# Gate and up projections of feed-forward tiles 3 to 20 as seven block products instead of eight

## The chip, the cores and the metric

The kernel runs on one core of one Trainium2 chip. The metric is the device time of one execution in microseconds (us).

## The reference, cut to what matters

Two encoder layers are computed for 576 tokens (512 of a prompt and 64 of a sample) of width 1024. Each layer has two feed-forward networks (FFNs), with a mixer and a cross attention between them. Only the FFNs are touched:

```
def swiglu(x, w_gate, w_up, w_down):
    return (jax.nn.silu(x @ w_gate) * (x @ w_up)) @ w_down

x = layer_norm(ALPHA * x + 0.5 * swiglu(x, ffn1_gate, ffn1_up, ffn1_down), g[0], b[0])
...
x = layer_norm(ALPHA * x + 0.5 * swiglu(x, ffn2_gate, ffn2_up, ffn2_down), g[3], b[3])
```

D_MODEL is 1024 and D_FF 2816, all in fp32.

## The kernel before, in words

Activations lie transposed, features on the partitions and the 576 tokens on the free axis, in halves of 288 (HT). Every fp32 operand is split into a rounded part hi and a rest lo, and a product is three matmuls: hi by hi, hi weights by lo tokens, lo weights by hi tokens (`passes`, L394, and `passes_half`, L406, for one half). Weights come as units of 128x1024, in one stream by SP into the ring `w_raw` of three buffers (L2226). SP loads a buffer again once its unit is split. Pool splits every unit (`unit`, L2124): one TENSOR_SCALAR writes the hi part (L2135), four TENSOR_TENSORs the lo part (L2142), into one of 12 slots. `unit_done` tells Pool that a slot is free, `unit_split` tells PE that a unit is there.

An FFN has 22 tiles of 128 hidden features and 66 units: a gate and a up unit for each tile, and two down units for two tiles. There are three stages:

- **Head** (`head`, L457): tiles 0 to 2, first for token half 0, then for half 1, while VectorE (DVE) and ScalarE (ACT) still normalise half 1. Its banks are those of `pairD` and one each of `pairA` and `pairB`.
- **Bodies** (`ffn`, L562): a tile is a `proj` of gate into pairA (48 matmuls of 288 columns) and one of up into pairB (48). ACT takes the silu of the gate, DVE multiplies it with up (L1591), ACT rounds the hidden tile to hi (L1103), and DVE makes its lo (L1595). Between two tiles stands a `down` of 96 matmuls over the two tiles before, in eight groups of 12 that alternate between pairD0 and pairD1. DVE adds each group to `y` (L1609).
- **Tail** (`tail`, L472): tile 21 and the last two down products by token half. Then `norm_of_ffn` runs: ACT squares `y`, Pool sums the squares (`squares_sum`, L2157), and `stats` (L586) on PE averages the sums over the partitions, between the gate and the up product of half 1.

What sets the order is the order of the program on each engine, with semaphores between them. Pool's is:

```
                ffn_units(0)
                units(mix, mix + HEAD)
                squares_sum(0, 0)
                squares_sum(0, 1)
```

so that before the squares of an FFN come the last units of its tail and the first six of the stage behind it. Only after the last FFN do none follow.

## Time and profile before

| | |
|---|---|
| median of three runs | 2674.93 us (2664.05 to 2677.69) |
| span of the profiled execution | 2675.5 us (no other time of that execution is given) |
| PE busy | 2556.2 us (96%), 18450 matmuls |
| DVE busy | 1056.0 us (39%) |
| ACT busy | 583.9 us (22%) |
| Pool busy | 1542.6 us (58%) |
| granted TensorE clock, mean | 0.972 of full speed |

The span runs from the first instruction to the last. Busy time is the union of an engine's instructions, and matmuls overlap: one lasts about 299 ns in the record, while they start closer together than that. The last section of rows gives what the argument needs, in groups with numbers.

### The profile page before, as it was taken

The page shows a single profiled execution, that of the slowest core. Times are in us where ns is not written, and L with a number is a line of the kernel's source. Part 1 is how long each engine was busy: PE and PEld are TensorE (multiplying, and loading weights), DVE is VectorE, ACT ScalarE, POOL GpSimd, SP SyncE. Part 2 cuts the span into 40 slices and gives each one's busy share as a digit, 9 for nine tenths or more (in the row PEclk, how much of TensorE's full clock was granted, in tenths as well). Part 3 has the DMA queues.
Part 4 walks back from the last instruction along what each step waited for, and adds up shares of the span by engine and source line. Part 5 has one row for each costly group of instructions (what it writes and reads, how often), then busy time and mean ns, then how long its engine had stood idle before and what let it go on. Part 6 is the DMA issues. An engine that isn't in the chain of part 4 may idle for free.

```text
span 2675.5 us, 47942 instructions
## 1 busy us (share of the span) xinstructions
PE 2556.2 (96%) x18450; PEld 2444.5 (91%) x18450; DVE 1056.0 (39%) x1601; ACT 583.9 (22%) x1096; POOL 1542.6 (58%) x1877
## 2 busy tenths in 40 slices
PE   8999999999988899999999999999999879999997
PEld 7999999978767799999999999999787768999997
DVE  3222225654647622222422222256445575222224
ACT  2000004422315500000320000044223254000004
POOL 8866662733239686666486666626332588766641
PEclk9999999989979999999999999999889999999999
DMA  6322220212113132222132222202121121322201
GB/s 229 118 79 86 79 86 9 80 48 71 52 48 95 57 113 81 85 80 84 40 114 87 83 82 80 83 2 87 40 89 35 64 97 64 103 87 78 85 33 36
DMA packets 61099, 203.99 MB, mean 76 GB/s; under 512 B 6808, under 2 KB 13976, under 8 KB 60312
## 3 DMA queue, kind: packets, MB, share of 16 engines
q1 hardware_dynamic: 52288, 184.83, 21.3%
q10 hardware_dynamic: 8664, 17.17, 1.8%
q8 instruction: 96, 1.57, 0.2%
q14 instruction: 51, 0.42, 0.1%
HBM read 195.66 MB, written 7.88 MB: 76 GB/s over the span
## 4 chain that ended last, share of the span: by engine, by line
PE 84%; DVE 9%; POOL 3%; issue 3%; ACT 1%; DMA 0%; DVEq 0%; POOLq 0%; ACTq 0%
PE pairA L401 22%; PE pairD L401 20%; PE pairB L401 19%; PE pairD L410 8%; PE pairA L410 2%; PE pairB L410 2%; POOL scratch L2175 1%; PE pairD L671 1%; PE pairD L673 1%; POOL w L2142 1%; DVE prx L2098 1%; DVE scratch L1816 1%; DVE y L1634 1%; PE pairD L793 0%; PE pairB L828 0%
## 5 line engine op out<-in xcount | busy, mean ns | idle before, releaser
L2142 POOL TENSOR_TENSOR w<-w_raw,w 128x256 fp32r<-128x256 f32 x1372 | 1044.2, 792 | 28.6
L2135 POOL TENSOR_SCALAR w<-w_raw 128x1024 fp32r<-128x1024 f32 x343 | 365.3, 1065 | 808.3 <-issue 450.0
L401 PE MATMUL pairA<-x_hi,w 128*128 128x288 f32 x3136 | 570.3, 299 | 3.6 <-DVE scratch L1564 2.7
L401 PE MATMUL pairB<-x_hi,w 128*128 128x288 f32 x2752 | 497.1, 298 | 0.0
L401 PE MATMUL pairD<-h_hi,w 128*128 128x288 f32 x2688 | 481.0, 298 | 16.0 <-DVE kw L1906 6.3
L401 PEld LDWEIGHTS pairA<-x_hi,w 128*128 128x128 f32 x3136 | 473.9, 191 | 7.0 <-issue 6.1
L401 PEld LDWEIGHTS pairD<-h_hi,w 128*128 128x128 f32 x2688 | 403.8, 191 | 18.9 <-issue 8.4
L401 PEld LDWEIGHTS pairB<-x_hi,w 128*128 128x128 f32 x2752 | 413.9, 191 | 1.1 <-issue 0.2
L1609 DVE TENSOR_TENSOR y<-y,pairD 128x576 f32<-128x576 f32 x256 | 193.1, 754 | 561.6 <-PE pairD L401 561.6
L401 PE MATMUL pairA<-x_lo,w 128*128 128x288 f32 x1568 | 339.1, 298 | 0.0
L401 PE MATMUL pairB<-x_lo,w 128*128 128x288 f32 x1376 | 297.2, 298 | 0.0
L401 PE MATMUL pairD<-h_lo,w 128*128 128x288 f32 x1344 | 290.6, 298 | 0.0
L1103 ACT ACTIVATE h_hi<-scratch 128x576 fp32r<-128x576 f32 x72 | 49.4, 686 | 956.5 <-DVE scratch L1591 956.5
L401 PEld LDWEIGHTS pairA<-x_lo,w 128*128 128x128 f32 x1568 | 256.2, 191 | 0.0
L401 PEld LDWEIGHTS pairB<-x_lo,w 128*128 128x128 f32 x1376 | 223.7, 191 | 0.0
L401 PEld LDWEIGHTS pairD<-h_lo,w 128*128 128x128 f32 x1344 | 218.3, 190 | 0.0
L2175 POOL TENSOR_TENSOR scratch<-scratch 128x288 f32<-128x288 f32 x112 | 98.6, 880 | 192.9 <-ACT scratch L1120 188.9
L410 PE MATMUL pairD<-x_hi,w 128*128 128x288 f32 x832 | 175.7, 303 | 22.0 <-DVE w L1520 12.4
L1591 DVE SCALAR_TENSOR_TENSOR scratch<-scratch,pairB 128x576 f32<-128x576 f32 x72 | 54.0, 751 | 339.8 <-PE pairB L401 339.8
L410 PEld LDWEIGHTS pairD<-x_hi,w 128*128 128x128 f32 x832 | 138.0, 192 | 24.9 <-issue 19.6
L410 PE MATMUL pairD<-h_hi,w 128*128 128x288 f32 x768 | 158.4, 298 | 2.3 <-DVE h_lo L1770 2.3
L410 PEld LDWEIGHTS pairD<-h_hi,w 128*128 128x128 f32 x768 | 124.6, 188 | 4.7 <-DVE h_lo L1770 3.2
(340 smaller groups left out, 2925.0 us busy)
## 6 DMA issues: line engine op xcount, KB each, us to landing
w_raw<-in_stream SPq DMA_DIRECT2D x348, 512.0 KB, 3.4
out_ak<-pa ACTq DMA_DIRECT2D x2, 1152.0 KB, 4.7
out_y<-y SPq DMA_DIRECT2D x8, 288.0 KB, 2.2
mem_raw<-in_mem ACTq DMA_DIRECT2D x2, 1024.0 KB, 4.7
cst<-in_consts ACTq DMA_DIRECT2D x1, 1740.0 KB, 8.2
tb_dram<-in_rel ACTq DMA_DIRECT2D x2, 768.0 KB
y<-in_x ACTq DMA_DIRECT2D x2, 576.0 KB, 7.0
y<-in_x ACTq DMA_DIRECT2D x1, 1152.0 KB, 11.2
```

The costliest lines, as they stand in the source:

```text
L401: ins.append(mm(out[0:m, half, 0:n], wt, mv_[:, c:c + n], start=(start and i == 0), stop=(stop and i == 2)))
L410: return [mm(out[:, 0:HT], wt, mv_[:, c], start=(start and i == 0), stop=(stop and i == 2)) for i, (wt, mv_) in enumerate(((wh, hi), (wh, ...
L671: i = mm(o[m, cols], lhs, dT[:, h, tok], start=True, stop=(t == 0))
L673: i = mm(o[m, cols], cs[r, p, st, 0:w], qw[r, p, tok], start=False, stop=True)
L1103: f(hs[t % 4][0], hf[:, 0:TOK], ACT.Copy).then_inc(h_hi_done.sem, 1)
L1591: v.scalar_tensor_tensor(out=both(hf[:, 0:TOK]), in0=both(sil[t % 2][:, 0:TOK]), scalar=0.5, in1=B.halves(), op0=ALU.mult, op1=ALU.mult).t ...
L1609: v.tensor_tensor(both(y[:, n]), both(y[:, n]), pair.halves(), ALU.add)\
L1634: v.scalar_tensor_tensor(out=y[:, n, half(h)], in0=y[:, n, half(h)], scalar=scalar, in1=t[:, 0:HT], op0=ALU.mult, op1=ALU.add).then_inc(us ...
L1816: step(v.reciprocal(r_, r_))
L2135: pool.tensor_scalar(hi, w_raw[:, j], 1.0, 0.0, ALU.mult, ALU.add).then_inc(unit_hi, 1)
L2142: i_ = pool.tensor_tensor(lo[:, b], w_raw[:, j, b], hi[:, b].bitcast(F32), ALU.subtract)
L2175: pool.tensor_tensor(s2[:, c], a[:, c], sil[n % 2][:, c], ALU.add)\
```

## The change

For tiles 3 to 20 of each FFN the gate and up products become one two-by-two block product. The weights have the blocks A11 and A12 (rows 0 to 511 and 512 to 1023 of gate) and two of up, the tokens are cut by rows and by token halves, and seven products of 12 matmuls on 288 columns take the place of eight. Four of the weight blocks are sums (S1 to S4), four of the token blocks too (T1 to T4, made once for an FFN). One call of `tile_pair` issues the seven products P1 to P7 of one tile, in the order of its `part` calls; P5, P6 and P7 add to the banks of P1, P3 and P4.

- **DVE** makes the weight sums of each tile (4 operations of 128x512), the lo parts of all seven blocks (7 of 128x512), five combinations of the products (128x288, one operand in PSUM), the hidden tile and its lo. It still adds the down groups. Its order is that of `half_body(k)`, which covers tiles t = 2k+3 and r = 2k+4. The sums and lo parts of tile t+2 stand within tile r, those of tile r within tile t and the down.
- **ACT** rounds the seven blocks to hi (7 of 128x512), copies P1 out of its bank (`keep_m1`), and takes silu by halves.
- **Pool** splits only the down units of the bodies, head and tail units as before. `pair_split` waits for DVE's three lo parts of the raw blocks, then releases both raw buffers.
- The homes of split weights change: two sets of seven blocks for alternating tiles, two slots for down units. Four of the six tail units lie over T1 to T4 and wait for the last products of tile 20.
- The loads of `gw_raw` and `lru_w` move from the first FFN to its norm, since they share memory with the blocks.

```diff
--- before.py
+++ after.py
-SLOTS = 12
-HEAD, TAIL, BODY = 6, 6, 12
-BODIES = (FFN_UNITS - HEAD - TAIL - 6) // BODY
...
+A11, S2, S1, S3, A12, S4, A22 = range(7)
+SUMS = (S1, S3, S2, S4)
+T2, T1, T3, T4 = range(4)
+SETS = (("e0", "e1", "e2", "sc", "b0", "b1", "b2"), ("b3", "b4", "b5", "b6", "b7", "b8", "b9"))
+D_SLOTS, TAIL_SLOTS = (5, 8), (9, 8, 10, 11, 12, 13)
+TAIL_OVER = {62: 2, 63: 3, 64: 4, 65: 7}
...
+    ffn = list(range(HEAD)) + HALVES * ["x", "x", *D_SLOTS, "y", "y"] + list(TAIL_SLOTS)
+    mixer = [i if i < HEAD else (i - HEAD) % 5 for i in range(MIX_UNITS + X_UNITS - 3)] + [HEAD - 1, 6, 7]
...
+                def tile_pair(u, t, fi, off=0):
+
+
+                    q = fi * PAIRS + t - 3
+                    at = pair_counts(l, q, off)
+                    first = t == 3
+                    blocks = sets[(t - 3) % 2]
+                    x_ = [[(x_hi[:, 4 * k:4 * k + 4, h * HT:h * HT + HT], x_lo[:, 4 * k:4 * k + 4, h * HT:h * HT + HT])
+                           for h in range(2)] for k in range(2)]
+
+                    def part(bank, b, src, start):
+                        (wh, wl), (hi, lo) = blocks[b], src
+                        ins = []
+                        for k in range(4):
+                            for i_, (wt, mv_) in enumerate(((wh, hi), (wh, lo), (wl, hi))):
+                                ins.append(mm(bank.t[:, 0:HT], wt[:, k], mv_[:, k], start=(start and k == i_ == 0),
+                                              stop=(k == 3 and i_ == 2), skip_group_check=not start))
+                        ins[-1].then_inc(product.sem, 1)
+                        return ins[0]
+
+                    unit_there(u + 1, BODY * off)
+                    if not first:
+                        pe.wait_ge(gate_on.sem, at(gate_on, 2, -1))
+                    tell_over(part(A.bank[0], A11, x_[0][0], True))
+                    if first:
+                        pe.wait_ge(tx_ready.sem, tx_ready.value(l, 4 * fi + 4))
+                    else:
+                        pe.wait_ge(combined.sem, at(combined, 5, -4))
+                    pe.wait_ge(sum_lo.sem, at(sum_lo, 4, 3))
+                    part(A.bank[1], S2, tx[T2], True)
+                    if not first:
+                        pe.wait_ge(combined.sem, at(combined, 5, -1))
+                    part(B.bank[0], S1, tx[T1], True)
+                    if not first:
+                        pe.wait_ge(combined.sem, at(combined, 5, 0))
+                    part(B.bank[1], S3, tx[T3], True)
+                    pe.wait_ge(m1_kept.sem, at(m1_kept, 1, 1))
+                    part(A.bank[0], A12, x_[1][0], False)
+                    pe.wait_ge(sum_lo.sem, at(sum_lo, 4, 4))
+                    pe.wait_ge(combined.sem, at(combined, 5, 2))
+                    part(B.bank[0], S4, x_[1][1], False)
+                    pe.wait_ge(combined.sem, at(combined, 5, 3))
+                    part(B.bank[1], A22, tx[T4], False)
+                    units_over(2)
...
                     with pe.Fori(0, BODIES) as i:
                         for m in range(2):
                             u = u0 + 12 + 6 * m
-                            proj(u, A, None, 12 * i, 4 * i, a0 + 2 * m)
-                            proj(u + 1, B, None, 12 * i, 4 * i, b0 + 2 * m)
+                            tile_pair(u, 5 + 2 * m, fi, i)
                             down(u + 2, h0 + 7 + 2 * m, None, 4 * i, 8 * i, (d0 + 4 * m, d1 + 4 * m), slot=2 - 2 * m)
-                            proj(u + 4, A, None, 12 * i, 4 * i, a0 + 2 * m + 1)
-                            proj(u + 5, B, None, 12 * i, 4 * i, b0 + 2 * m + 1)
...
                     hi_half(fi, FT - 1, 1)
+                    if fi == 0:
+                        load_mixer()
...
+                    y_ = [[y[:, 4 * k:4 * k + 4, half(h)] for h in range(2)] for k in range(2)]
+                    raw = tx_f
+                    inc(v.tensor_tensor(raw[T1], y_[0][0], y_[0][1], ALU.subtract), tx_made)
+                    inc(v.tensor_tensor(raw[T3], y_[0][1], y_[1][1], ALU.subtract), tx_made)
+                    dve.wait_ge(tx_made.sem, tx_made.value(l, 4 * fi + 1))
+                    inc(v.tensor_tensor(raw[T2], y_[1][1], raw[T1], ALU.add), tx_made)
+                    dve.wait_ge(tx_made.sem, tx_made.value(l, 4 * fi + 3))
+                    inc(v.tensor_tensor(raw[T4], y_[1][0], raw[T2], ALU.subtract), tx_made)
...
+                def sums(fi, t, first, off=0):
+
+                    u = fi * FFN2_AT + 2 * t + 2 * ((t - 3 + 1) // 2)
+                    at = pair_counts(l, fi * PAIRS + t - 3, off)
+                    g, up = raw_pair(u)
+                    raw = sums_f[(t - 3) % 2]
+                    if first == 0:
+                        raw_there(dve, l, u, off)
+                        raw_there(dve, l, u + 1, off)
+                        room(dve, l, u, off)
+                        v.tensor_tensor(raw[S1], up[:, 0:4], up[:, 4:8], ALU.add).then_inc(sum_made.sem, 1)
+                        v.tensor_tensor(raw[S3], g[:, 0:4], up[:, 0:4], ALU.add).then_inc(sum_made.sem, 1)
+                    else:
+                        dve.wait_ge(sum_made.sem, at(sum_made, 4, 1))
+                        v.tensor_tensor(raw[S2], raw[S1], g[:, 0:4], ALU.add).then_inc(sum_made.sem, 1)
+                        dve.wait_ge(sum_made.sem, at(sum_made, 4, 3))
+                        v.tensor_tensor(raw[S4], raw[S2], g[:, 4:8], ALU.add).then_inc(sum_made.sem, 1)
...
+                    m6, m5, m7 = (b.t[:, 0:HT] for b in (A.bank[1], B.bank[0], B.bank[1]))
+                    if n == 0:
+                        dve.wait_ge(m1_kept.sem, at(m1_kept, 1, 1))
+                    dve.wait_ge(product.sem, at(product, 7, (2, 3, 4, 6, 7)[n]))
+                    if n in (1, 2):
+                        dve.wait_ge(combined.sem, at(combined, 5, n))
...
+                    out, a, b, op = ((v_, m6, kept, ALU.subtract), (up1, v_, m5, ALU.subtract), (up1, up1, m7, ALU.add),
+                                     (g1, m5, v_, ALU.subtract), (up0, v_, m7, ALU.add))[n]
+                    v.tensor_tensor(out, a, b, op).then_inc(combined.sem, 1)
...
                 def ffn(fi, h0):
                     for h in range(2):
                         for t in range(3):
+                            if (h, t) == (0, 2):
+                                tokens_made(fi)
                             hidden_half(fi, t, h)
-                    a0, b0 = uses[("ffn", fi, "A")], uses[("ffn", fi, "B")]
+                            if (h, t) == (0, 2):
+                                tokens_lo(fi)
+                            if (h, t) == (1, 0):
+                                sums(fi, 3, 0)
+                                sums(fi, 3, 2)
+                            if (h, t) == (1, 1):
+                                raws_lo(fi, 3, (0, 1, 2))
+                                for n in range(4):
+                                    sums_lo(fi, 3, n)
...
+                    def half_body(k, off=0):
+                        t, r = 2 * k + 3, 2 * k + 4
+                        more = k + 1 < HALVES
+                        combine(fi, t, h0, 0, off)
+                        combine(fi, t, h0, 1, off)
+                        combine(fi, t, h0, 2, off)
+                        if k:
+                            sums(fi, r, 0, off)
+                            raws_lo(fi, r, (0, 1), off)
+                        combine(fi, t, h0, 3, off)
+                        if k:
+                            sums(fi, r, 2, off)
+                        combine(fi, t, h0, 4, off)
+                        hidden(fi, t, off)
+                        if k == 0:
+                            hidden_lo(fi, t, h0, off)
+                            sums(fi, r, 0)
+                            raws_lo(fi, r, (0, 1))
+                            sums(fi, r, 2)
+                        for n in range(KT):
+                            down_add(k, n, off)
+                            if n == 1:
+                                if k:
+                                    hidden_lo(fi, t, h0, off)
+                                raws_lo(fi, r, (2,), off)
+                            if 2 <= n < 6:
+                                sums_lo(fi, r, n - 2, off)
+                        if more:
+                            sums(fi, t + 2, 0, off)
+                        combine(fi, r, h0, 0, off)
+                        if more:
+                            sums(fi, t + 2, 2, off)
+                        combine(fi, r, h0, 1, off)
+                        combine(fi, r, h0, 2, off)
+                        if more:
+                            raws_lo(fi, t + 2, (0, 1, 2), off)
+                        combine(fi, r, h0, 3, off)
+                        if more:
+                            sums_lo(fi, t + 2, 0, off)
+                        combine(fi, r, h0, 4, off)
+                        if more:
+                            sums_lo(fi, t + 2, 1, off)
+                        hidden(fi, r, off)
+                        if more:
+                            sums_lo(fi, t + 2, 2, off)
+                        hidden_lo(fi, r, h0, off)
+                        if more:
+                            sums_lo(fi, t + 2, 3, off)
...
+                    if SLOT[w] in TAIL_SLOTS[2:]:
+                        pool.wait_ge(product.sem, product.value(l, 7 * ((w // FFN2_AT + 1) * PAIRS - 1)
+                                                                + TAIL_OVER[w - w // FFN2_AT * FFN2_AT]))
...
+                def pair_split(u, fi, t, off=0):
+
+                    at = pair_counts(l, fi * PAIRS + t - 3, off)
+                    pool.wait_ge(raw_lo.sem, at(raw_lo, 3, 3))
+                    pool.wait_ge(unit_split, l * UNITS + u + BODY * off)
+                    pool.sem_inc(unit_split, 2)
...
+                    def half_body(k, off=0):
+                        u = at + HEAD + HALF * k
+                        pair_split(u, fi, 2 * k + 3, off)
+                        unit(u + 2, off)
+                        unit(u + 3, off)
+                        pair_split(u + 4, fi, 2 * k + 4, off)
```

Three places in the order of the instructions follow. First VectorE inside the loop, in the second tile of a half body, behind its last raw lo part. `e` and `w` are homes of blocks, `sc_lo` too, `e_0f` and `w_0f` the unrounded sums, and `scratch` holds the combinations and the hidden tile (L1853). Now:

```order
L1846 TENSOR_TENSOR scratch<-pairB,scratch 128x288 [waits product]
L1815 ISA
L1817 TENSOR_TENSOR e<-e_0f,e 128x512 [waits block_hi]
L1846 TENSOR_TENSOR scratch<-scratch,pairB 128x288 [waits product]
L1815 ISA
L1817 TENSOR_TENSOR sc_lo<-scratch,sc_hi 128x512 [waits block_hi]
L1851 ISA
L1852 ISA [waits gate_on]
L1853 SCALAR_TENSOR_TENSOR scratch<-scratch 128x576 [waits combined]
L1815 ISA
L1817 TENSOR_TENSOR e<-e_0f,e 128x512 [waits block_hi]
L1858 ISA
```

The second L1846 waits for P7, and the third L1817 makes the lo part of S2 for the next tile. Before, DVE had here only L1591 and L1595.

Second PE, at the start of the next tile, the products P1 and P2 (`tq` are the token sums). Now:

```order
L674 ISA [waits unit_split]
L667 MATMUL pairA<-x_hi,e 128x288 [waits gate_on]
...
L679 ISA
L680 ISA [waits combined]
L667 MATMUL pairA<-tq,e 128x288 [waits sum_lo]
L667 MATMUL pairA<-tq,e 128x288 x11
L683 ISA
```

P2 begins when the lo part of S2 is there. Before, the gate product of a tile stood here, with one wait at its start.

Third Pool, from the end of its loop to the squares of the first norm. Now:

```order
L2470 TENSOR_SCALAR e<-w_raw 128x1024
L2477 TENSOR_TENSOR e<-w_raw,e 128x256 x4
L2470 TENSOR_SCALAR d<-w_raw 128x1024
L2477 TENSOR_TENSOR d<-w_raw,d 128x256 x4
L2470 TENSOR_SCALAR t<-w_raw 128x1024
L2477 TENSOR_TENSOR t<-w_raw,t 128x256 x4
...
L2470 TENSOR_SCALAR w<-w_raw 128x1024
L2477 TENSOR_TENSOR w<-w_raw,w 128x256 x4
...
L2527 TENSOR_TENSOR scratch<-scratch 128x288 x14
```

The t units are four and the w units six. Before, all twelve were w units in the same order; what moved is when their homes come free. The d unit (61) goes where the last down unit (57) was, which is free from P1 of tile 20 on, and behind it stand ten more units.

## Rows read from the trace of the kernel before

**Rows 1.** The page, part 1: busy time of the engines.
```profile
PE 2556.2 (96%) x18450; PEld 2444.5 (91%) x18450; DVE 1056.0 (39%) x1601; ACT 583.9 (22%) x1096; POOL 1542.6 (58%) x1877
```

**Rows 2.** Chain that ended last: start us, us, what. The downs of one FFN.
```profile
66.83 12.80 PE pairD L401 x96
105.17 12.80 PE pairD L401 x96
```

**Rows 3.** Stretch of a head: us, busy by PE, PEld, DVE, ACT, POOL, PEclk, DMA, GB/s.
```profile
1364.27:1377.07 12.80, 12.80 (x98) 12.80 (x97) 1.90 (x4) 1.72 (x4) 5.97 (x9) 1.00 0.18 53
```

**Rows 4.** Durations: by lines (mean ns after busy) or by source (ns min/median/max).
```profile
L1634 DVE SCALAR_TENSOR_TENSOR y<-y,pairD 128x288 f32<-128x288 f32 x128 | 54.3, 445 | 29.0 <-PE pairD L410 29.0
L1609 DVE TENSOR_TENSOR y<-y,pairD 128x576 f32<-128x576 f32 x256 | 193.1, 754 | 561.6 <-PE pairD L401 561.6
L1968 DVE TENSOR_TENSOR pc<-pc,scratch x8: 757/759/1186, 645.3 to 2132.0; 128x576 f32<-128x576 f32 x8
L1831 DVE TENSOR_TENSOR yd<-yd,scratch x4: 1109/1146/1186, 503.9 to 1858.5; 128x512 f32<-128x512 f32 x4
L2142 POOL TENSOR_TENSOR w<-w_raw,w x1372: 716/737/1720, 6.0 to 2583.5; 128x256 fp32r<-128x256 f32 x196
L1103 ACT ACTIVATE h_hi<-scratch 128x576 fp32r<-128x576 f32 x72 | 49.4, 686 | 956.5 <-DVE scratch L1591 956.5
```

**Rows 5.** Timeline of DVE at a tile's end: start us, us, what, [idle before].
```profile
309.81 0.76 DVE L1609 TENSOR_TENSOR y<-y,pairD 128x576 f32<-128x576 f32 x1 [0.84 <-PE pairD L401]
310.48 0.75 DVE L1591 SCALAR_TENSOR_TENSOR scratch<-scratch,pairB 128x576 f32<-128x576 f32 x1
311.98 1.30 DVE L1595 TENSOR_TENSOR h_lo<-scratch,h_hi 128x576 fp32r<-128x576 f32 x1 [0.75 <-ACT h_hi L1103]
```

**Rows 6.** Timeline of DVE, three heads, and of PE: tile 3.
```profile
35.37 0.60 DVE L1572 TENSOR_TENSOR h_lo<-scratch,h_hi 128x288 fp32r<-128x288 f32 x1 [0.51 <-ACT h_hi L1079]
...
927.68 0.60 DVE L1572 TENSOR_TENSOR h_lo<-scratch,h_hi 128x288 fp32r<-128x288 f32 x1 [0.51 <-ACT h_hi L1079]
...
948.27 0.50 PE L401 MATMUL pairA<-x_hi,w 128*128 128x288 f32 x2 [0.89 <-DVE scratch L1564]
...
1359.17 0.81 DVE L1572 TENSOR_TENSOR h_lo<-scratch,h_hi 128x288 fp32r<-128x288 f32 x1 [0.51 <-ACT h_hi L1079]
```

**Rows 7.** Timeline of PE and POOL: the first tail, and two units behind each other.
```profile
400.59 0.37 PE L410 MATMUL pairA<-x_hi,w 128*128 128x288 f32 x1 [1.36 <-DVE scratch L1591]
...
422.87 0.65 PE L606 MATMUL pairA<-scratch,cst 128*128 128x288 f32 x2
...
413.81 0.81 POOL L2175 TENSOR_TENSOR scratch<-scratch 128x288 f32<-128x288 f32 x1 [8.35 <-ACT scratch L1120]
...
420.96 0.81 POOL L2175 TENSOR_TENSOR scratch<-scratch 128x288 f32<-128x288 f32 x1 [0.74 <-ACT scratch L1120]
...
933.70 1.05 POOL L2135 TENSOR_SCALAR w<-w_raw 128x1024 fp32r<-128x1024 f32 x1
...
937.84 1.05 POOL L2135 TENSOR_SCALAR w<-w_raw 128x1024 fp32r<-128x1024 f32 x1
```

**Rows 8.** The page, part 6: DMA issues, KB each, us to landing.
```profile
w_raw<-in_stream SPq DMA_DIRECT2D x348, 512.0 KB, 3.4
```

**Rows 9.** Timeline of PE: three matmuls behind an idle time.
```profile
553.00 0.24 PE L719 MATMUL pairD<-cst,scratch 4*128 4x4 f32 x1 [1.96 <-DVE scratch L1862]
...
694.24 0.40 PE L401 MATMUL pairD<-h_hi,w 128*128 128x288 f32 x1 [1.73 <-DVE pr L2008]
...
1342.75 0.58 PE L410 MATMUL pairD<-x_hi,w 128*128 128x288 f32 x1 [3.40 <-POOL w L2142]
```

**Rows 10.** Stretches behind the idle times of rows 9, columns as in rows 3.
```profile
553.00:559.40 6.40, 6.40 (x18) 3.16 (x19) 2.15 (x6) 3.00 (x7) 0.35 (x1) 0.50 0.04 14
694.20:700.60 6.40, 6.36 (x48) 6.37 (x48) 3.01 (x4) 0.87 (x2) 3.88 (x5) 1.00 0.07 12
1342.75:1357.95 15.20, 15.20 (x96) 15.20 (x97) 7.67 (x11) 9.45 (x16) 14.87 (x17) 0.82 0.37 113
```

More of the change, by code:

```diff
@@ L94, with unit_homes @@
-SLOT, BEFORE = slot_table()
+HEAD, TAIL, HALF = 6, 6, 6
+HALVES = (FFN_UNITS - HEAD - TAIL) // HALF
+BODY = 2 * HALF
+BODIES = (HALVES - 1) // 2
+PAIRS = 2 * HALVES
+FFN_H = 6 + PAIRS + 2
+A11, S2, S1, S3, A12, S4, A22 = range(7)
[4 more added lines that the diff above has]
+TAIL_OVER = {62: 2, 63: 3, 64: 4, 65: 7}
+def unit_homes():
+    parts = {i: (f"b{2 * i}", f"b{2 * i + 1}") for i in range(5)}
+    parts |= {5: ("d0",), 6: ("t0",), 7: ("t1",), 8: ("d1",), 9: ("e0", "e1")}
+    parts |= {10: ("t0",), 11: ("t1",), 12: ("t2",), 13: ("t3",), "x": SETS[0], "y": SETS[1]}
+    ffn = list(range(HEAD)) + HALVES * ["x", "x", *D_SLOTS, "y", "y"] + list(TAIL_SLOTS)
+    mixer = [i if i < HEAD else (i - HEAD) % 5 for i in range(MIX_UNITS + X_UNITS - 3)] + [HEAD - 1, 6, 7]
+    table = ffn + mixer + ffn
+    held = dict.fromkeys([q for p in parts.values() for q in p], -UNITS)
+    for turn in range(2):
+        over = []
+        for u, home in enumerate(table):
+            second = home in ("x", "y") and over and u % 2
+            over.append(over[-1] if second else max(held[q] for q in parts[home]))
+            for q in parts[home]:
+                held[q] = u
+        held = {q: u - UNITS for q, u in held.items()}
+    return table, over
@@ L95 @@
+SLOT, BEFORE = unit_homes()
 for at_ in (0, FFN2_AT):
-    for u_ in range(at_ + HEAD + 6, at_ + FFN_UNITS - TAIL):
-        assert SLOT[u_] == SLOT[u_ - BODY] and BEFORE[u_] == u_ - BODY
+    for u_ in range(at_ + HEAD + HALF, at_ + FFN_UNITS - TAIL):
+        assert BEFORE[u_] == u_ - HALF + (SLOT[u_] in ("x", "y") and u_ % 2 == 0)
 CONST_COLS = [("ident", P), ("ones", P), ("avg", P), ("blk", P), ("perm", P), ("mask", P), ("cos", TOK), ("sin", TOK),
@@ L1111, in ffn @@
+                    half_body(0)
+                    with act.Fori(0, BODIES - 1) as i:
+                        half_body(1, i)
+                        half_body(2, i)
+                    half_body(HALVES - 2)
+                    half_body(HALVES - 1)
+                    h_hi_done.n += PAIRS
                     silu_half(fi, FT - 1, 0)
@@ L2214, in _ @@
             s2_added.n, stats_ready.n = 8 * (KT - 2), 8
+            for c, per in ((product, 7), (m1_kept, 1), (combined, 5), (gate_on, 2), (h_made, 1), (block_hi, 7),
+                           (sum_made, 4), (sum_lo, 4), (raw_lo, 3)):
+                c.n = 2 * PAIRS * per
             y_added.n, E("y_summed").n = 2 * (KT - 2), 7
```

318 lines of the change are left out of this document (222 added, 96 removed), and 4 rows, old and new, of the table COUNTS.

## The prediction

> **What bounds the kernel now.** I read the busy shares first: TensorE is busy 96% of the span, VectorE 39%, Pool under 60% [rows 1]. So the kernel ends when the matmuls end, and the other engines cost nothing as long as they keep pace. The chain of waits confirms it in the FFN: two downs of 96 matmuls stand 38.34 us apart with 288 matmuls between their starts, 0.1331 us each [rows 2], so nothing is lost there. A group of 12 is 1.60 us. The half-width form costs the same: 96 of the head's take 12.80 us [rows 3]. Fewer matmuls shorten the span only where every wait that replaces them stays below the work before it. So I replay each engine's order, with durations from [rows 4].
>
> **Removed.** 4 FFNs x 18 tiles x (96 - 84) = 864 matmuls x 0.1331 = **-115.0 us**. A half body then takes 264 matmuls = 35.1 us.
>
> **Prices.** A VectorE operation with one PSUM operand takes 0.445 us at 288 columns and 0.754 at 576; two SBUF operands at 576 take 0.757 with Pool idle and up to 1.186 beside it [rows 4]. The block operations (two SBUF operands, 512 columns) don't occur in the FFN before. From above stands 1.146 us, 512 wide beside a working Pool [rows 4]; from below about 0.69, by the slope between 288 and 576 columns. An operation that needn't wait starts 0.67 us after one of 0.76 [rows 5], so back to back 0.61 us. VectorE starts about 0.04 us after Pool, ACT or its own result, and 0.2 us after the start of the first matmul behind a product. PE's first matmul comes 0.35 us after VectorE's end (947.92 to 948.27 in [rows 6], the multiply there being 0.45 long).
> The Trainium skill ("SBUF — State Buffer", Who interferes with whom) calls the port that both share an exclusive lock, held for the whole instruction. The rows show less: the slowed operation takes 1.3 us at most [rows 5], where a full Pool operation of 0.74 in front would make 1.5. By the lock each of the three contended operations below would cost some 0.3 us more, 30 us over the kernel. I go by the rows, and keep this in the upper bound.
>
> **The wait at P2.** P2 of tile t+2 needs the lo part of S2, which VectorE makes after P7 of tile r. From P7's end: 0.2 us to the start, combination 0.45, lo of S3, hidden (576), lo of S2, and 0.35 to PE. Idle Pool: 0.2 + 0.4 + 0.6 + 0.7 + 0.7 + 0.35 = 2.95 us, P1 covers 1.60, leaving 1.35. But Pool is not idle: `pair_split` holds it until the last raw lo part, which in tile r comes at about 8.9 us (after P4 at 6.6 and three operations). Then it splits both down units for over 8 us, across all of this. Contended the three operations take about 1.05, 1.2 and 1.1, sum 4.1 us, leaving **2.5 us**. That happens for tiles 5, 7, ... 19: 8 x 4 x 2.5 = **+80 us** (bounds 43 and 110). The other waits are covered: m1 copy and combinations have 4.8 us or more (three products) or 3.2 (two), and VectorE holds 10 us of work against the down's 12.8.
>
> **The first down.** With k = 0 VectorE does tile 4's sums before the down's first addition: after P7 0.2 + 0.45 + hidden 0.8, ACT's hi 0.7, lo 0.8, then four sums and two raw lo parts, 3.8, and an addition 0.75, in all 7.5, + 0.35 to PE. The two pairs of D give 3.2 us of cover: 4.6 x 4 = **+18 us**.
>
> **The head.** VectorE gets there only after its norm; its second lo of half 0 ends at 928.28, 35.97 and 1359.98 [rows 6]. From there to the release of tile 3 it now has four token differences of 1152 columns (1.36 each by the same slope, 5.3), tile 2 with ACT in between 2.1, four token lo parts 5.2, tile 0 of half 1 1.4, four weight sums 2.7, ACT's queue 1.5, tile 1 1.4, seven lo parts 4.4, tile 2 0.45: 24.4 us, + 0.35. That gives 953.0 against 948.27 [rows 6]: +4.8, in both second FFNs. In the first FFN it gives 60.7 against 54.0, which is 66.83 less a tile's 12.8 [rows 2]: +6.7. In layer 2's first FFN it gives 1384.7, where PE's half 1 from 1364.27 [rows 3] with its 144 matmuls and the wait behind them ends at 1384.6: nothing. **+16 us**. Pool rests meanwhile, held by `pair_split`.
>
> **The tail.** A unit takes Pool 4.14 us [rows 7]. The new slots let it start unit 61 only at P1 of tile 20; behind it stand units 62 to 65 and six of the next stage: 11 x 4.14 = 45.5 us. The tail starts 12.3 us after P1 (seven products, then the last combination), so Pool begins the squares 33.3 us into the tail, where it began at 13.2 (413.81 - 400.59) [rows 7]. They take 7 to 8 us (413.81 to 421.77), so `stats` gets them at 41; PE asks at 22.3 [rows 7]. 18.7 us, in three tails (behind the last FFN no units stand): **+56 us**. The tail's own start waits 1.36 us now [rows 7] and then 0.2 + 0.45 + 0.35 less the overlap of matmuls, 0.9: **-2 us**. SP's ring should keep up: two buffers wait for `pair_split`, but by the order a load is then released 6 us or more ahead of its use, and lands in 3.4 [rows 8].
>
> **The clock.** A pause of 1.73 us left the granted clock at 1.00, one of 1.96 was followed by 0.50, after 3.40 us 96 matmuls took 15.2 us at 0.82 instead of 12.8 [rows 3, 9, 10]. So the long pauses (4 first downs, 3 heads, 3 tails) cost 10 x 2.4 = **+24 us**. The 32 pauses at P2 lie between these rows: from 0 to 2.4 us each, 0 to 77 in all. Since 1.96 already was followed by the half clock once and 1.73 not, I take 1.0 each: **+32 us**.
>
> The mixer and cross attention are the same. The moved loads of `gw_raw` and `lru_w` have a whole norm half and a head before their use, so nothing.
>
> **Sum.** -115 + 80 + 18 + 16 + 56 - 2 + 24 + 32 = **+109 us**. On the profiled span of 2675.5 us, 0.6 above the median of 2674.93, that gives **2784 us**, 4.1% slower.
>
> **Rivals.**
> 1. *Pool and VectorE don't meet, or the clock doesn't mind* (0.22). If Pool is late by a few us, or the contended operations are nearer 0.7, the pause is 1.35 us, below 1.73, and the clock holds: 2784 - 37 - 32 = **2715 us**. For: VectorE's operations with PSUM are not slowed at all beside Pool, 0.445 and 0.754. Against: L1595 beside Pool took 1.30 [rows 5].
> 2. *VectorE is the bound* (0.10). Its work per half body is 22 block operations, 10 combinations, 8 additions, 4 of 576: 29 us beside an idle Pool, 34 if Pool slows half of it, 39 if all. At 35.1 of PE time little is left, and every pause grows: 2 us more in 32 half bodies and a clock drop in each, **2860 us**.
> 3. *The pause at P2 is covered* (0.08), on the other side. It decides whether the lo part of S2 is ready 1.25 us after P7's end. If VectorE's order lets it be, 112 us go: **2672 us**, no change. For: VectorE's whole time fits. Against: combination, lo, hidden and lo stand behind P7 in its order, and alone need 2.6. If the tail's wait is smaller too (squares that ACT has prepared go faster), it is faster: 2640 (0.04).
> 4. *Pool doesn't hold the tail* (0.08 for this alone): 2784 - 56 - 7 = **2721 us**. Against: the order has ten units behind unit 61, and each needs four slow operations.
> 5. *The change doesn't do what it says*: the seven products issue 12 matmuls of the same form each, so only a slower matmul would void the gain; the head's rate says no [rows 3].
>
> **How the numbers follow.** My case has 0.48 and spans 2745 to 2825 by the bounds of the P2 pause and the clock. Cases 1 and 4 (0.30) lie at 2715 to 2721, case 2 (0.10) above, cases 3 (0.12) below. A range of 2705 to 2835 leaves out case 3 and most of case 2, 2 in 10. A measurement here tells 0.5%, 13 us, from no change. Faster by more is only the second half of case 3, 0.04; within 0.5% the rest of it, 0.08; slower 0.88.
>
> **What would show it.** In the changed kernel's profile PE has 864 matmuls fewer. In the timeline PE idles 2.5 us before P2 of every second tile, released by L1817 of VectorE, with L1817 and L1853 at 1.1 to 1.2 us; 4 to 5 us before a third group of the first down, released by the addition; and some 19 us before `stats` in three tails, released by Pool's squares. The granted clock is at 0.5 in stretches inside the bodies, where it is 1.00 now. The prediction is wrong if Pool's units in the tail come before P1 of tile 20, if P2's pause is under 1.5 us, or if busy TensorE stays at 1.00.

## The result, and the profile after

The changed kernel takes 2775.8 us (median of four runs, 2772.0 to 2782.3), the kernel before 2674.1 beside it: ratio 1.039, 95% interval 1.037 to 1.042. Forecast were 2784 us, with a range of 2705 to 2835. The profiled execution took 2776.3 us, its span is 2774.4 and its mean granted clock 0.946; before it was 0.972. The span is 98.9 us longer; the prediction's sum was +109.

The page, part 1, beside [rows 1], and the row of part 5 for product P2:

```profile
PE 2495.9 (90%) x17586; PEld 2371.0 (85%) x17586; DVE 1799.6 (65%) x2785; ACT 919.1 (33%) x1760; POOL 1030.0 (37%) x1157
...
L667 PE MATMUL pairA<-tq,e 128*128 128x288 f32 x432 | 79.6, 342 | 76.5 <-DVE e L1817 76.5
```

PE has the 864 matmuls less, and stands idle for 10% of the span where it was 4%. The largest single piece is 76.5 us before P2, released by the lo part of S2 (L1817).

**The pause before P2.** Timeline of DVE and PE from P6 of a second tile to the next tile's P2 (start us, us, what, [idle before]):

```profile
1103.29 0.94 DVE L1817 TENSOR_TENSOR e<-e_0f,e 128x512 fp32r<-128x512 f32 x1
1104.52 0.45 DVE L1846 TENSOR_TENSOR scratch<-scratch,pairB 128x288 f32<-128x288 f32 x1 [0.29 <-PE pairB L667]
1104.89 1.19 DVE L1817 TENSOR_TENSOR sc_lo<-scratch,sc_hi 128x512 fp32r<-128x512 f32 x1
1106.01 1.29 DVE L1853 SCALAR_TENSOR_TENSOR scratch<-scratch 128x576 f32<-128x576 f32 x1
1107.22 1.22 DVE L1817 TENSOR_TENSOR e<-e_0f,e 128x512 fp32r<-128x512 f32 x1
...
1105.78 0.29 PE L667 MATMUL pairA<-x_hi,e 128*128 128x288 f32 x1
1108.49 0.40 PE L667 MATMUL pairA<-tq,e 128*128 128x288 f32 x1 [2.42 <-DVE e L1817]
```

P7's last matmul starts at 1104.18, P1's first at 1104.32 and its last at 1105.78. Behind the last combination (1104.52) VectorE makes a lo part, the hidden tile and a second lo part, and P2 starts 0.05 us after the last of them ends. It starts 2.71 us after P1's last, 2.58 later than a matmul that waits for nothing (0.13). Such a pause (2.26 to 2.80 us) stands in all 32 places; the sum of these excesses is 81.4 us. Pool works through it, and the lines of L1817 by target show what that does:

```profile
L1817 DVE TENSOR_TENSOR w<-w_0f,w x180: 677/685/1532, 59.4 to 2704.2; 128x512 fp32r<-128x512 f32 x180
L1817 DVE TENSOR_TENSOR e<-e_0f,e x72: 683/1030/1266, 57.6 to 2680.0; 128x512 fp32r<-128x512 f32 x72
L1817 DVE TENSOR_TENSOR sc_lo<-scratch,sc_hi x36: 682/1190/1293, 58.2 to 2677.8; 128x512 fp32r<-128x512 f32 x36
```

The same 128x512 subtraction takes 0.685 us alone and 1.19 to 1.22 in this place beside Pool. The combination with an operand in PSUM keeps its 0.45.

**First down, heads, tail.** Timeline of PE, five first matmuls behind a wait: tile 3 of the first FFN, of the second, and of layer 2's first; the third group of the first down; `stats` in the first tail.

```profile
60.67 0.60 PE L667 MATMUL pairA<-x_hi,e 128*128 128x288 f32 x1 [7.05 <-DVE scratch L1762]
984.94 0.60 PE L667 MATMUL pairA<-x_hi,e 128*128 128x288 f32 x1 [4.25 <-DVE scratch L1762]
1441.44 0.40 PE L667 MATMUL pairA<-x_hi,e 128*128 128x288 f32 x1 [0.82 <-DVE scratch L1762]
...
81.97 0.61 PE L488 MATMUL pairD<-h_hi,w 128*128 128x288 f32 x1 [4.08 <-DVE y L1881]
...
455.01 1.32 PE L736 MATMUL pairA<-scratch,cst 128*128 128x288 f32 x2 [17.98 <-POOL scratch L2527]
```

And of Pool from its unit 61 to the first squares, beside [rows 7]:

```profile
402.75 1.05 POOL L2470 TENSOR_SCALAR d<-w_raw 128x1024 fp32r<-128x1024 f32 x1 [3.43 <-issue]
...
445.35 2.76 POOL L2477 TENSOR_TENSOR w<-w_raw,w 128x256 fp32r<-128x256 f32 x4
448.07 0.79 POOL L2527 TENSOR_TENSOR scratch<-scratch 128x288 f32<-128x288 f32 x1
449.42 5.46 POOL L2527 TENSOR_TENSOR scratch<-scratch 128x288 f32<-128x288 f32 x6 [0.55 <-ACT scratch L1316]
```

**The clock.** Two stretches from one P2 pause to the next, columns as in [rows 3], with the same 267 matmuls:

```profile
1105.50:1143.30 37.80, 35.38 (x267) 35.15 (x266) 29.71 (x45) 11.52 (x22) 10.36 (x12) 1.00 0.24 85
297.50:336.90 39.40, 36.91 (x267) 36.68 (x266) 29.75 (x45) 11.52 (x22) 10.41 (x12) 0.96 0.23 81
```

Behind half of the pauses the half clock is granted for a short time, and each such time makes the way to the next pause 39.2 us long in place of 37.7. By these distances and the granted clock I count them in every kernel: here behind 16 of the 32 pauses of P2, 1.5 us each. The trace gives the whole cost of the clock by another way: TensorE works for 239 us of the span while the half clock is granted, and did so for 133 before. At half the clock a 288-column matmul starts 0.24 us behind the one before it and not 0.133, so 0.45 of such time is lost, 47 us of the difference of 106.

| term | predicted | measured |
|---|---|---|
| 864 matmuls | -115 | -115 (taken at 0.133 each) |
| wait before P2, 32 | +80 | +81.4 |
| first down, 4 | +18 | +17.0 |
| heads | +6.7, +4.8, +4.8, 0 | +6.1, +3.4, +3.4, -0.1 |
| stats in three tails | +56 | +54.6 |
| tail start, 4 | -2 | -1.8 |
| clock behind P2 pauses | +32 | +24 (16 x 1.5) |
| clock behind long pauses | +24 | +26 (not read, but the rest of 98.9, other stages in it; with the 24 above it is 50, against the 47) |

### The profile page after: what moved, and what is told of

Its sections match the earlier page's. It is cut to its first block, busy times and chain, and to the rows that moved or that the text cites. A ratio compares the mean times of both kernels' runs of the same rounds, so it can differ in the third digit from the quotient of the medians.

```text
span 2774.4 us, 49442 instructions
## 1 busy us (share of the span) xinstructions
PE 2495.9 (90%) x17586; PEld 2371.0 (85%) x17586; DVE 1799.6 (65%) x2785; ACT 919.1 (33%) x1760; POOL 1030.0 (37%) x1157
## 4 chain that ended last, share of the span: by engine, by line
PE 68%; DVE 15%; POOL 7%; issue 6%; ACT 3%; DVEq 0%; ACTq 0%; DMA 0%; POOLq 0%; SPq 0%
PE pairD L488 19%; PE pairB L667 16%; PE pairA L667 11%; PE pairA L488 5%; PE pairD L497 4%; POOL w L2477 3%; PE pairB L488 2%; POOL scratch L2527 2%; DVE scratch L1853 2%; DVE e L1817 1%; PE pairB L497 1%; PE pairD L801 1%; PE pairD L803 1%; POOL t L2477 1%; PE pairA L497 1%
## 5 line engine op out<-in xcount | busy, mean ns | idle before, releaser
L2470 POOL TENSOR_SCALAR w<-w_raw 128x1024 fp32r<-128x1024 f32 x139 | 148.0, 1065 | 1443.9 <-POOLq L2485 914.7
L2477 POOL TENSOR_TENSOR w<-w_raw,w 128x256 fp32r<-128x256 f32 x556 | 470.6, 876 | 11.6
L488 PE MATMUL pairD<-h_hi,w 128*128 128x288 f32 x1536 | 290.6, 307 | 32.4 <-DVE y L1881 16.3
L488 PEld LDWEIGHTS pairD<-h_hi,w 128*128 128x128 f32 x1536 | 241.1, 199 | 36.3 <-DVE y L1881 17.2
L667 PE MATMUL pairB<-tq,w 128*128 128x288 f32 x1728 | 247.5, 295 | 0.0
L667 PEld LDWEIGHTS pairB<-tq,w 128*128 128x128 f32 x1728 | 236.0, 188 | 0.0
L488 PE MATMUL pairD<-h_hi,d 128*128 128x288 f32 x1152 | 208.3, 296 | 0.5
L1846 DVE TENSOR_TENSOR scratch<-scratch,pairB 128x288 f32<-128x288 f32 x216 | 97.8, 453 | 146.0 <-PE pairB L667 145.9
L667 PE MATMUL pairA<-x_hi,w 128*128 128x288 f32 x864 | 188.1, 294 | 0.0
L488 PEld LDWEIGHTS pairD<-h_hi,d 128*128 128x128 f32 x1152 | 171.3, 188 | 3.2 <-DVE y L1887 3.2
L488 PE MATMUL pairA<-x_hi,w 128*128 128x288 f32 x832 | 159.8, 311 | 0.0
L1817 DVE TENSOR_TENSOR w<-w_0f,w 128x512 fp32r<-128x512 f32 x180 | 148.9, 827 | 0.0
L667 PE MATMUL pairA<-tq,e 128*128 128x288 f32 x432 | 79.6, 342 | 76.5 <-DVE e L1817 76.5
L667 PEld LDWEIGHTS pairA<-x_hi,w 128*128 128x128 f32 x864 | 143.9, 188 | 0.0
```

Source lines behind the costliest of these rows:

```text
L488: ins.append(mm(out[0:m, half, 0:n], wt, mv_[:, c:c + n], start=(start and i == 0), stop=(stop and i == 2)))
L667: ins.append(mm(bank.t[:, 0:HT], wt[:, k], mv_[:, k], start=(start and k == i_ == 0), stop=(k == 3 and i_ == 2), skip_group_check=not start))
L1817: v.tensor_tensor(lo, raw, hi.bitcast(F32), ALU.subtract).then_inc(sum_lo.sem, 1)
L1846: v.tensor_tensor(out, a, b, op).then_inc(combined.sem, 1)
L2470: pool.tensor_scalar(hi, w_raw[:, j], 1.0, 0.0, ALU.mult, ALU.add).then_inc(unit_hi, 1)
L2477: i_ = pool.tensor_tensor(lo[:, b], w_raw[:, j, b], hi[:, b].bitcast(F32), ALU.subtract)
```

## The experiments

Each is compared with the changed kernel's 2775.8 us; the kernel before ran beside all of them at 2672 to 2675, so medians of different sets can be set side by side. Trace readings are from one execution each, which is not always near the median: it is the fastest of four in e4_tail, e5_first_down and e8_tokens, and the slowest in e3_fill and e6_head. Each ratio is to the kernel before, with its 95% interval.

**1. The order behind P7** (e1_order):

```diff
+                        if more:
+                            sums_lo(fi, t + 2, 0, off)
                         combine(fi, r, h0, 3, off)
                         if more:
-                            sums_lo(fi, t + 2, 0, off)
+                            sums_lo(fi, t + 2, 1, off)
                         combine(fi, r, h0, 4, off)
                         if more:
-                            sums_lo(fi, t + 2, 1, off)
-                        hidden(fi, r, off)
-                        if more:
                             sums_lo(fi, t + 2, 2, off)
+                        hidden(fi, r, off)
                         hidden_lo(fi, r, h0, off)
```

> VectorE makes the lo parts of S1, S3 and S2 of tile t+2 before, between and behind the last two combinations of tile r, and the hidden tile after them. Theory A (the pause before P2 is the chain combination, lo, hidden, lo that stands behind P7 in VectorE's order): only the combination and one lo part are left, 0.20 + 0.37 + 1.2 + 0.05 = 1.8 us, of which P1 covers 1.6. The pause falls from 2.6 to about 0.2 us, 32 x 2.4 = 77 us less, and the 16 stretches at half clock behind these pauses, 1.5 us each, go too: 2776 - 77 - 24 = 2675 us. Theory B (VectorE's whole work in a half body, or Pool beside it, is what bounds): the pause comes back elsewhere, at P6 or in the down, and at most 30 us are gained: 2745 us or more.

2667.2 us, ratio 0.999 (0.997 to 1.001): 109 us less than the changed kernel, theory A. Its row for P2 and the timeline of the same place:

```profile
L667 PE MATMUL pairA<-tq,e 128*128 128x288 f32 x432 | 68.7, 309 | 2.1 <-DVE e L1817 0.5
```

```profile
1072.14 0.46 DVE L1846 TENSOR_TENSOR scratch<-scratch,pairB 128x288 f32<-128x288 f32 x1 [0.29 <-PE pairB L667]
1072.51 1.19 DVE L1817 TENSOR_TENSOR e<-e_0f,e 128x512 fp32r<-128x512 f32 x1
1073.63 1.30 DVE L1853 SCALAR_TENSOR_TENSOR scratch<-scratch 128x576 f32<-128x576 f32 x1
...
1073.76 1.87 PE L667 MATMUL pairA<-tq,e 128*128 128x288 f32 x12
```

Idle time before P2 falls from 76.5 us to 2.1; by starts of matmuls, P2 comes 0.2 us late in most places, 6.6 us in all. The operations beside Pool are as slow as before (1.19, 1.30), and that costs next to nothing, since only one of them is still in front of P2. VectorE has the same work in a shorter time, and no new wait came up. So nothing but the place of three lo parts in VectorE's order made the difference between 3.9% slower and no difference to the kernel before.

**2. Pool kept away from the three operations** (e2_late_pool):

```diff
                         pair_split(u, fi, 2 * k + 3, off)
+                        if k:
+                            pool.wait_ge(sum_lo.sem, pair_counts(l, fi * PAIRS + 2 * k, off)(sum_lo, 4, 3))
```

> Pool begins the down units of a half body only when the lo part of S2 is made (for k over 0); nothing else is changed. Theory A (the three operations are slow because Pool works beside them): lo, hidden and lo take 0.69, 0.76 and 0.69 us as everywhere else, the pause falls from 2.6 to about 1.0 us, 32 x 1.6 = 51 us less, and the clock drops behind it, 16 x 1.5, mostly go: 2776 - 51 - 24 = 2700 us. Theory B (they are slow for a reason of their own, such as their place behind ScalarE): the durations stay at 1.2 us, 2776 us. Theory C: the down units come too late for the down behind P7, a new wait there, between 2700 and 2776.

2789.5 us, ratio 1.041 (1.036 to 1.046). The durations went as A says:

```profile
L1817 DVE TENSOR_TENSOR e<-e_0f,e x72: 680/682/687, 56.8 to 2692.0; 128x512 fp32r<-128x512 f32 x72
L1817 DVE TENSOR_TENSOR sc_lo<-scratch,sc_hi x36: 682/685/686, 57.4 to 2690.7; 128x512 fp32r<-128x512 f32 x36
...
1070.97 1.86 PE L667 MATMUL pairA<-tq,e 128*128 128x288 f32 x12 [0.83 <-DVE e L1817]
```

P2 now starts 1.12 us behind P1's last matmul, not 2.71: Pool's company was worth 1.6 us of each pause, 51 us in all. But the time did not fall. C came in another form than I wrote: not the down units were late, but the raw weights. Pool's later start releases `w_raw` later, and in the middle of tile t VectorE stands idle for the next pair:

```profile
1079.83 0.69 DVE L1803 TENSOR_TENSOR w_0f<-w_raw 128x512 f32<-128x512 f32 x1 [3.17 <-DMA w_raw<-in_stream]
```

It is then late for the first additions, and PE waits 2.1 us in each of the 32 downs of the half bodies behind the first. These waits, less the normal step of 0.13, come to 32 x 2.1 = 66 us, which takes back the 51. The clock is hardly better (0.949): no half clock stands behind a pause of P2 any more, but one stands behind 13 of these 32 waits. The ring of three raw buffers was near its limit, which the prediction had passed over with "SP's ring should keep up". It does, but with less than Pool's delay to spare.

**3. The pause filled** (e3_fill):

```diff
+FILL = 16
...
+                    if t % 2 and not first:
+                        warm = 0
+                        while warm < FILL:
+                            (wh, wl), (hi, lo) = blocks[A11], x_[0][0]
+                            for k in range(4):
+                                mm(A.bank[1].t[:, 0:HT], wh[:, k], hi[:, k], start=True, stop=True)
+                                warm += 1
                     pe.wait_ge(sum_lo.sem, at(sum_lo, 4, 3))
```

> In the pause before P2 of every second tile PE issues 16 matmuls more into the bank that P2 then starts anew, 2.1 us of work in a pause of 2.6; they compute nothing that is used, and the pause ends when it did. Theory A (the half clock behind these pauses comes from the idle time): the 16 stretches at 0.50 go, 16 x 1.5 = 24 us less: 2752 us. Theory B (the stretches are not due to the pause, or cost nothing since PE waits again anyway): 2776 us. Theory C (the extra weight loads and matmuls delay P2): up to 10 us more than before, 2786 us.

2748.9 us, ratio 1.027 (1.022 to 1.031): 27 us less with 512 matmuls more. The distance between two P2 is 37.4 to 37.9 us everywhere in the four FFNs, never 39.2. So the half clock behind these pauses comes from PE's rest, and costs what its 16 times gave, 24 us, within the spread of the runs (2738 to 2756).

**4. The squares before the next stage's units** (e4_tail), and in the same way behind the second FFN:

```diff
-                units(mix, mix + HEAD)
                 squares_sum(0, 0)
+                units(mix, mix + 3)
                 squares_sum(0, 1)
-                units(mix + HEAD, cross - 5)
+                units(mix + 3, cross - 5)
```

> Pool sums the squares of half 0 before the six units of the next stage, and those of half 1 behind three of them. Theory A (Pool's queue alone holds stats): the wait of 18.3 us before stats goes in three tails, 55 us, and the half clock behind it, 3 x 2.1 us: 2776 - 61 = 2715 us. Theory B (what was in front of the squares is now late itself): units 4 to 6 of the next stage or the sum for half 1 hold PE, and of the 18.3 us 8 or more come back in each: 2740 us or more.

2707.1 us, ratio 1.013 (1.009 to 1.016): 69 us less. No wait is left before `stats` of half 0: Pool has its sums done before PE asks. For half 1 Pool is back in time, and PE waits 0.5 us there at most:

```profile
426.97 0.81 POOL L2527 TENSOR_TENSOR scratch<-scratch 128x288 f32<-128x288 f32 x1 [4.32 <-ACT scratch L1316]
...
434.15 0.80 POOL L2527 TENSOR_TENSOR scratch<-scratch 128x288 f32<-128x288 f32 x1 [0.75 <-ACT scratch L1316]
...
448.23 0.81 POOL L2527 TENSOR_TENSOR scratch<-scratch 128x288 f32<-128x288 f32 x1 [0.90 <-ACT scratch L1316]
```

Pool even waits for ScalarE's squares, at both halves. Theory A, and 8 us more than it said, which lies within what the clock gives and takes by chance (experiment 7).

**5. The first down's additions first** (e5_first_down): with k = 0, behind each of the first four additions stands one piece of what was in front of them, and the lo parts of the sums behind the last four:

```diff
-                        if k == 0:
-                            hidden_lo(fi, t, h0, off)
-                            sums(fi, r, 0)
-                            raws_lo(fi, r, (0, 1))
-                            sums(fi, r, 2)
                         for n in range(KT):
                             down_add(k, n, off)
+                            if k == 0 and n < 4:
+                                (lambda: hidden_lo(fi, t, h0), lambda: sums(fi, r, 0), lambda: sums(fi, r, 2),
+                                 lambda: raws_lo(fi, r, (0, 1, 2)))[n]()
+                            if k == 0 and n > 3:
+                                sums_lo(fi, r, n - 4)
...
```

> With k = 0 VectorE adds each group of the first down before it goes on with tile 4's sums and lo parts, one or two of them between two additions. Theory A (the wait in the first down is VectorE's order): the 4.4 us before the third group go, 4 x 4.2 = 17 us, and the half clock behind them, 3.2 + 1.5 + 3.2 + 1.5 = 9 us: 2776 - 26 = 2750 us. Theory B (11 block operations and 8 additions don't fit beside a down of 12.8 us): the wait moves to P1 or P2 of tile 4, 2 to 4 us each time: 2762 us or more.

2744.9 us, ratio 1.028 (1.025 to 1.031): 31 us less, theory A. One wait of 0.6 us is left in this down, behind the three raw lo parts that I put together, and none at tile 4:

```profile
84.77 0.53 PE L488 MATMUL pairD<-h_hi,d 128*128 128x288 f32 x2 [0.61 <-DVE y L1881]
```

**6. Lo parts out of the head** (e6_head):

```diff
                                 raws_lo(fi, 3, (0, 1, 2))
-                                for n in range(4):
-                                    sums_lo(fi, 3, n)
+                    for n in range(4):
+                        sums_lo(fi, 3, n)
```

> The four lo parts of the sums of tile 3 stand behind the last hidden tile of the head, not before it. Theory A (VectorE's queue ends the head): P1 starts 2.4 us earlier, but P2 then waits for three lo parts, 1.8 us behind the release, of which P1 covers 1.6; the three long head pauses (6.1, 3.4, 3.4 us over those of before) shrink by about 2.2 us each: 2776 - 7 = 2769 us. Theory B (something else ends the head, such as ScalarE or a load): no change in these pauses, 2776 us.

2772.2 us, ratio 1.036 (1.033 to 1.039): nothing that can be told from the changed kernel. Neither theory had it. P1 did come 2.4 us earlier, but then P2 waited, longer than A's arithmetic allows:

```profile
57.91 0.60 PE L667 MATMUL pairA<-x_hi,e 128*128 128x288 f32 x1 [4.66 <-DVE scratch L1762]
62.61 0.61 PE L667 MATMUL pairA<-tq,e 128*128 128x288 f32 x1 [1.46 <-DVE e L1817]
...
58.69 1.04 POOL L2470 TENSOR_SCALAR w<-w_raw 128x1024 fp32r<-128x1024 f32 x1 [36.12 <-PE pairA L667]
...
58.76 1.52 DVE L1817 TENSOR_TENSOR e<-e_0f,e 128x512 fp32r<-128x512 f32 x1
60.20 1.22 DVE L1817 TENSOR_TENSOR sc_lo<-scratch,sc_hi 128x512 fp32r<-128x512 f32 x1
61.34 1.21 DVE L1817 TENSOR_TENSOR e<-e_0f,e 128x512 fp32r<-128x512 f32 x1
```

P1 of tile 3 frees the slot for which Pool had waited since the head began, so Pool starts exactly when the moved lo parts do. Three of 0.6 us became three of 1.2 to 1.5. In all, the three long heads gave 7.2 us before P1, and P2 of tile 3 lost 9.9 us over four heads, since it came late also in layer 2's first FFN, where P1 had nothing to gain.

**7. The four orders together** (e7_all):

> The orders of e1_order, e4_tail, e5_first_down and e6_head together; the seven products stay. If the terms are independent, as the prediction's sum has it: 2776 - 101 - 61 - 26 - 7 = 2581 us, 3.5% under the kernel before. If VectorE or the weight loads bound a half body once the pauses are gone (22 block operations, 10 combinations, 8 additions and 4 wide ones against 35.1 us): about 2650 us. If the removal of 864 matmuls were not worth its 115 us: 2675 us or more.

2592.2 us, ratio 0.970 (0.967 to 0.973): **3% faster than the kernel before**. The page:

```profile
PE 2454.5 (95%) x17586; PEld 2332.2 (90%) x17586; DVE 1811.3 (70%) x2785; ACT 918.3 (35%) x1760; POOL 1029.5 (40%) x1157
```

The waits are nearly independent, and VectorE at 70% is no bound. The four single gains are 109, 69, 31 and 4 us, 212 together; the common kernel gained 184. The waits that went and those that stayed are the same in the records; the clock is what differs. TensorE's work at the half clock, 239 us in the changed kernel, fell by 76, 40 and 71 us in e1_order, e4_tail and e5_first_down and grew by 12 in e6_head, 174 less together; here it fell by 97, to 142. Of the 77 us between them 0.45 is lost time, 34 us, and the 28 us that are missing fit in it. How often the half clock is granted varies from kernel to kernel and run to run: behind the 32 pauses of P2 there were 14 in e4_tail, 16 in e5_first_down, 13 in e6_head, and 9 in the next kernel, whose four runs span 2742 to 2766 us with mean clocks of 0.956 to 0.945. So I estimate that a single gain contains up to some 10 us of chance, and e4_tail's 8 us too much and e5_first_down's 5 are within that.

**8. A better head** (e8_tokens). What PE needs first stays in front; T3, T4 and S4 follow, and PE waits for each where it is used (the same for P7 with `4 * fi + 4`):

```diff
-                                tokens_lo(fi)
+                                tokens_lo(fi, (0, 2))
...
-                                for n in range(4):
+                                for n in range(3):
                                     sums_lo(fi, 3, n)
+                    tokens_lo(fi, (1, 3))
+                    sums_lo(fi, 3, 3)
...
-                        pe.wait_ge(tx_ready.sem, tx_ready.value(l, 4 * fi + 4))
+                        pe.wait_ge(tx_ready.sem, tx_ready.value(l, 4 * fi + 2))
...
+                    if first:
+                        pe.wait_ge(tx_ready.sem, tx_ready.value(l, 4 * fi + 3))
                     part(B.bank[1], S3, tx[T3], True)
```

> The order of the changed kernel except in the head: the lo parts of T3 and T4 and of S4 are made behind the last hidden tile, and PE asks for them only before P4, P7 and P6; the lo parts of S1, S3, S2, T1 and T2 stay in front. Theory A (VectorE's queue in front of the release ends the head): two lo parts of 1.35 us and one of 0.6 leave it, the three long head pauses fall from 7.35, 4.54 and 4.54 us to 4.1, 1.3 and 1.3, and unlike in e6_head nothing waits behind, since P4 comes 4.8 us after P1 even where Pool slows the three: 2776 - 10 = 2766 us, and up to 6 less by the clock. Theory B (work that is moved back is paid at the next product, as in e6_head): the pauses shrink but P4 or P7 waits 2 us or more: 2774 us.

2751.2 us, ratio 1.031 (1.027 to 1.034). Tile 3 of the first FFN and of the second:

```profile
57.22 0.60 PE L667 MATMUL pairA<-x_hi,e 128*128 128x288 f32 x1 [3.91 <-DVE scratch L1766]
...
966.85 0.39 PE L667 MATMUL pairA<-x_hi,e 128*128 128x288 f32 x1 [1.11 <-DVE scratch L1766]
```

The pauses fell by 3.1 us in each of three heads, as A says, and no product of tile 3 waits. That explains 9.4 us. The profiled run, the fastest of four, is 33.8 us shorter than the changed kernel's; the other 24 us lie within what the clock gave, since TensorE works 56 us less at half of it, which is 25 us of lost time. Of these, 10.5 us are the seven drops less behind P2 pauses (16 - 9), with which the edit has nothing to do. What the shorter heads brought by the clock is not shown. So theory A rests on the waits in the trace and not on the median, which is 24.6 us less.

**9. The best version** (e9_all):

> e7_all with the head of e8_tokens in place of that of e6_head. Theory A: e7_all lost 6.6 us in three long heads and 6.7 us before P2 of tile 3 over the rest; both nearly go, 2592 - 10 = 2582 us, in any case 3% or more under the kernel before. Theory B: the head costs the same wherever its VectorE work stands: 2592 us.

2587.9 us, ratio 0.967 (0.964 to 0.970). The waits before P1 and P2 of tile 3 are as in e8_tokens. In the records 10.7 us of waits are gone against e7_all. The median is only 4.3 us less, which the intervals don't tell from nothing; that it is 3.3% faster than the kernel before, they do.

## Why the prediction was right, step by step

The time came out 8 us under the forecast, and the waits stood where the prediction put them. Two sizes were off, the clock at P2 and the second heads; one was right partly by luck, the pause at P2.

- **Removed**: 864 matmuls, 115 us. The seven products run at 0.133 us a matmul. e7_all bears the price out: of 115 us, 80 arrive against the 2672 us beside it, and what was left over explains about 30 of the other 35 (5.5 us in heads, 8.7 before P2 of tile 3, 7 in the small rest before each P2, 3 in first downs, and 4 to 8 of clock). So rival 5, a change that doesn't do what it says, fell too.
- **The wait at P2**: the chain and its owner were right, 81.4 us against 80. The terms as they stand in the text add up to 4.3 us and not the 4.1 written. Measured from P1's first matmul (P7's end there) are 0.20 + 0.37 + 1.12 + 1.21 + 1.27 = 4.17. Errors met that cancel: the contended operations take up to 0.15 us more than I gave them, and PE follows VectorE's end by 0.05 us, not the 0.35 that I read from [rows 6]. So the mechanism was right, and that the 2.5 us fit so well was partly luck.
- **What stood against the lock**: while Pool makes its four lo parts from 1103.78 on (4.07 us, 2.82 alone), VectorE does work worth about 1.9 us alone (0.61, 0.67 and, in part, 0.3 in front and 0.3 behind). An exclusive lock held for the whole instruction, as the Trainium skill has it ("SBUF — State Buffer", Who interferes with whom), would need 4.7 us for both. The measurement decides: they overlap in part. But the overlap is small. Where both always have work, VectorE starts an operation every 1.12 to 1.22 us and Pool one every 1.13 to 1.22 (1105.49, 1106.63, 1107.85), and one of each behind the other would take 0.61 + 0.70 = 1.31. So they nearly take turns, and the three operations took 3.55 us from start to start where the forecast had 3.35: of the 30 us extra that the prediction set down for the lock, some 6 came. Which part of an instruction excludes the other was not tried.
- **First down, tail, tail start**: 17.0, 54.6 and -1.8 us against 18, 56 and -2. Pool's eleven units took from 402.75 to 448.07, 45.3 us against 45.5.
- **Head**: the count was right (from 36.35, the end of the second lo, to 60.67 are 24.3 us; from 960.48 to 984.94 are 24.5; I had 24.75). But in the second FFNs PE itself reached the end of its head 1.1 us later behind this lo than before (19.9 against 18.8 us), so that only 3.4 of the 4.8 us showed.
- **The clock**: 24 us behind the P2 pauses against 32; the size was off because I gave each pause a mean price. It is 1.5 us or nothing, and in this run it was half and half. e3_fill shows the cause. That an idle time of about 1.9 us can be followed by the half clock and need not be, which the prediction took from two rows, is borne out by e2_late_pool: 13 of 32. The long pauses' 24 us are near the 26 left over; they were not measured one by one.
- **Rival 1** (the operations don't meet or the clock doesn't mind) fell with L1817's 1.2 us and the stretches at 0.96, its "for" was true all the same: operations with PSUM are not slowed. **Rival 2** fell: VectorE has 29.7 us of work in 37.8, and e1_order took 2.4 us from each half body without a new wait. Its 2860 us do not follow from its words (2784 + 32 x 2 + 32 x 1.4 is 2893); both lie above the range. **Rival 3** did not happen but is what e1_order built: I gave 2672 us for it, and it took 2667. **Rival 4** is e4_tail, 2707 against 2721.

What the prediction did not see is that the sum of its own waits could all be ordered away: it lists them as the price of the change, and they were the price of four places in two engines' orders.

## What to carry to other kernels

When products are traded for sums and combinations on another engine, the time is decided by what stands between the last operand's arrival and the one result PE asks for next: put that result first, and everything that is needed a product later behind it. Before units of a later stage are queued on a helper engine, look for the small reduction behind them that the critical engine asks for. And where two engines slow each other on SBUF, count which of the slowed operations is in front of a wait, not how many there are; moving one engine's work away in time may only hit the buffer ring that it releases.

## What the runs showed of the hardware

- A VectorE subtraction of 128x512 with both operands in SBUF takes 0.685 us alone, and 1.21 in the median of the 98 that ran wholly beside Pool in the changed kernel (in e6_head 1.52, where Pool's 128x1024 TENSOR_SCALAR ran at its start). Pool's own 128x256 operation goes from 0.74 to 1.18 in the median where such VectorE operations run all the time. A VectorE operation that reads PSUM keeps its 0.455 at 128x288: 135 wholly beside Pool and 215 beside none have the same median. I had expected 1.05 to 1.2 us; that it can reach 1.5 behind a wide Pool operation was new.
- The half clock behind a pause of 2.6 us is granted in some cases and not in others, of the same kernel and the same place in the loop: 16, 14, 16, 13 and 9 of 32 in five kernels with the same pauses. Behind the 32 pauses of e2_late_pool at the same place, 1.12 us long, there were none; behind its 32 waits in the downs, with 1.9 us of idle time each, there were 13.
